# A two-block model step on one core: how the head normalises its inputs, how keys, values and gates are projected, and where three small steps of the feed-forward tail stand

## The reference, cut to what matters

```python
ada_x = split(silu(c) @ w_ada + b_ada, 6);  ada_c = split(silu(c_ctx) @ w_ada + b_ada, 6)
hc = rmsnorm(ctx, g) * (1 + ada_c[1]) + ada_c[0]       # modulated inputs
hx = rmsnorm(x, g)   * (1 + ada_x[1]) + ada_x[0]
pc = hc @ w_in[:, q|k|v|gates] + b_in                  # keys, values, gates of both streams
px = hx @ w_in + b_in
h = sin(z @ w1 + b1); h = sin(h @ w2 + b2); h = h @ w3 # filter chain, 256 x 2048
k = concat(h_forward * decay, h_backward * decay)      # its spectrum multiplies that of the input
...
x = x + g_f * ((silu(gt) * up) @ w_ffn_out)            # twice; the last result is the output
```

## Time and profile before

| | |
|---|---|
| median of three runs (lowest, highest) | 2293.68 us (2292.12, 2294.32) |
| the profiled execution: its own time, its span | 2291.01 us, 2289.2 us |
| busy: TensorE, its weight loads, DVE, ACT | 1917.2 (84%), 1260.9 (55%), 694.3 (30%), 337.6 (15%) us |
| chain that ended last: TensorE, DMA, DVE, ACT | 59%, 33%, 5%, 1% |
| HBM read | 646.10 MB, 283 GB/s over the span |
| 600 to 900 us (experts): DMA share, rate | 1.01, 429 GB/s |

### The profile page before, as it was taken

The page is one execution under the profiler, slowest core; times in us unless marked ns, Lnnn a source line. Parts: engine busy times, 40 slices in busy tenths (PEclk is TensorE's granted clock), DMA queues, the critical chain, the costliest instruction groups (busy, mean ns, idle before and its releaser), DMA issues.

```text
span 2289.2 us, 29892 instructions
## 1 busy us (share of the span) xinstructions
PE 1917.2 (84%) x12646; PEld 1260.9 (55%) x12646; DVE 694.3 (30%) x1643; ACT 337.6 (15%) x776; POOL 0.2 (0%) x4
## 2 busy tenths in 40 slices
PE   7999998966666666666666679999999999999998
PEld 4468687621111111111111137868889978688888
DVE  4113234300000000000000025562656545625554
ACT  3231021200000000000000010260210102602100
POOL 0000000000000000000000000000000000000000
PEclk9999999987878878787878789999999999999999
DMA  9245568999999999999999995524644555246441
GB/s 351 78 146 208 207 246 296 403 429 427 429 428 428 429 428 427 430 427 430 427 430 427 429 405 180 173 75 166 239 165 163 183 189 183 76 166 239 155 158 56
DMA packets 147883, 648.60 MB, mean 283 GB/s; under 512 B 10645, under 2 KB 17410, under 8 KB 123016
## 3 DMA queue, kind: packets, MB, share of 16 engines
q1 hardware_dynamic: 143956, 643.74, 71.1%
q10 hardware_dynamic: 3828, 3.43, 0.5%
HBM read 646.10 MB, written 1.05 MB: 283 GB/s over the span
## 4 chain that ended last, share of the span: by engine, by line
PE 59%; DMA 33%; DVE 5%; ACT 1%; issue 1%; SPq 0%; ACTq 0%; DVEq 0%
DMA ring<-in_w_exp 33%; PE bank L1842 15%; PE bank L825 14%; PE bank L2525 5%; PE bank L1625 4%; PE bank L1377 4%; PE bank L2440 2%; PE bank L1640 2%; PE bank L839 1%; PE bank L858 1%; PE bank L703 1%; DVE scr L2351 1%; PE bank L595 1%; PE bank L1302 1%; PE bank L1311 1%
## 5 line engine op out<-in xcount | busy, mean ns | idle before, releaser
L1625 PE MATMUL bank<-ring,arena 128*32 128x512 f32 x1968 | 309.3, 763 | 205.1 <-DMA ring<-in_w_exp 194.8
L825 PE MATMUL bank<-hx,ring 128*128 128x256 f32 (+1 forms) x1408 | 322.3, 390 | 0.7 <-ACT hx L721 0.7
L1625 PEld LDWEIGHTS bank<-ring,arena 128*32 128x32 f32 x1968 | 61.1, 124 | 436.0 <-DMA ring<-in_w_exp 315.6
L825 PEld LDWEIGHTS bank<-hx,ring 128*128 128x128 f32 x1408 | 267.8, 191 | 53.3 <-issue 18.8
L1640 PE MATMUL bank<-ring,arena 128*32 128x512 f32 x1008 | 157.9, 765 | 81.8 <-DMA ring<-in_w_exp 71.0
L1683 DVE COPY arena<-bank 128x256 f32<-128x256 f32 x16 | 6.8, 425 | 523.8 <-PE bank L1630 523.8
L1842 PE MATMUL bank<-arena 128*128 128x256 f32 x672 | 151.0, 379 | 0.3 <-DVE arena L1891 0.3
L1640 PEld LDWEIGHTS bank<-ring,arena 128*32 128x32 f32 x1008 | 32.1, 129 | 191.6 <-DMA ring<-in_w_exp 113.7
L1842 PEld LDWEIGHTS bank<-arena 128*128 128x128 f32 x672 | 127.0, 190 | 17.5 <-DVE arena L1891 0.6
L1690 DVE COPY arena<-bank 128x256 f32<-128x256 f32 x16 | 6.8, 425 | 343.5 <-PE bank L1514 343.5
L1842 PE MATMUL bank<-ring,hx 128*128 128x256 f32 x448 | 105.8, 379 | 0.0
(11 more groups left out here) (446 smaller groups left out, 2224.7 us busy)
## 6 DMA issues: line engine op xcount, KB each, us to landing
ring<-in_w_exp SPq DMA_DIRECT2D x186, 2048.0 KB, 16.2
ring<-in_w_ada SPq DMA_DIRECT2D x36, 2048.0 KB, 12.1
ring<-in_w_in SPq DMA_DIRECT2D x29, 2048.0 KB, 8.9
ring<-in_w_ffn_in SPq DMA_DIRECT2D x20, 2048.0 KB, 8.0
ring<-in_w_ffn_out SPq DMA_DIRECT2D x10, 2048.0 KB, 7.7
ring<-in_w_out SPq DMA_DIRECT2D x6, 2048.0 KB, 10.9
arena<-in_w_exp SPq DMA_DIRECT2D x4, 2048.0 KB, 19.3
ring<-in_w_up_nsa SPq DMA_DIRECT2D x2, 2048.0 KB, 7.8
```

The costliest lines, as they stand in the source:

```text
L825: ins = pe.matmul(b[:, o:o + n], w[:, k, j * P:(j + 1) * P], h[:, k, :], start=k == 0, stop=k == KD - 1)
L1625: ins = pe.matmul(banks[s][32 * j:32 * j + 32, :], e_xe[:, 2 * t + kk, :], w[:, kk, 512 * j:512 * j + 512], start=t + kk == 0, stop=t + kk ...
```

## The change

Seven edits in one. (1) The head's squares are summed by ACT on the token rows as they arrive (`act_stats`), the rows are scaled there (`act_normed`), and only then turned (`turnxn`, `turncn`); `x` is also turned raw, since it is needed later. The sums over ones on TensorE are gone. ACT modulates `x` and DVE `ctx` in one operation a block. (2) The identity matrix is loaded first, and the filter's tables are issued at the start by ACT. (3) The filter chain is ahead of the tables and the modulation; the taps come in an order that completes the first filter early; five spectra stand ahead of the modulation, two within it, three behind it. (4) Keys and values are made by seven half-size products each (`pe_seven_wide`), with DVE making T and S and combining the results. (5) The gate products go to four column groups of TensorE, and the picks of the gates' rows do too, behind the queries. (6) `dve_late` stands ahead of the second tile's sums. (7) In the last tile of `pe_down` m5 stands ahead of m7, and only one quarter of the result is turned ahead of the last products. The core of the diff:

```diff
+        load("load_ident", ident[:, :], A["k_ident"])
...
-    def act_dft_loads(act):
         act_load(act, "load_decay", decay, A["k_decay"])
         act_load(act, "load_dft", skips, A["hy_skip"].rearrange("a o n -> a (o n)"))
...
+    def dve_gate_pad(v):
+        DV.stage("project")
+        v.wait_ge(*K.loaded("load_ident"))
+        v.memset(wgate, 0.0).then_inc(*DV.step())
+        v.memset(bgate, 0.0).then_inc(*DV.step())
+        v.tensor_tensor(fold0, ident[:, 0:32], ident[:, 32:64], ALU.add).then_inc(*DV.step())
+        for i in (64, 96):
+            v.wait_ge(*DV.last())
+            v.tensor_tensor(fold0, fold0, ident[:, i:i + 32], ALU.add).then_inc(*DV.step("gate pad"))
...
+        for c, a in TAPS:
+            key = f"filter h{c}{a}"
+            v.wait_ge(*at("full " + key))
+            b = bank_of(key)
+            v.tensor_tensor(hfil[:, c, a, :], b[:, :], decay[:, c, a % 2, :], ALU.mult).then_inc(*DV.step("free " + key))
+            if a % 2:
+                o = a // 2
+                v.wait_ge(*DV.last())
+                v.tensor_tensor(hsd[c][o][:, 0, :], hfil[:, c, a - 1, :], hfil[:, c, a, :], ALU.add).then_inc(*DV.step())
...
+            if t == 2:
+                pe_spectra(pe, 1, (0, 1))
+                PE.stage("ada")
...
+    def act_stats(act, src, load, i):
+        AC.stage("stats")
+        act.wait_ge(*K.loaded(load))
+        for c in range(NC):
+            junk = (mg[:, 1024:2048], mg[:, 2048:3072], mg[:, 3072:4096], scr[:, 0:1024])[i + c]
+            act.activation(junk, src[:, c, :], ACT.Square, accum_out=st[:, i + c:i + c + 1]).then_inc(*AC.step("stats"))
...
+    def act_normed(act, key, src, i, read):
+        AC.stage("stats")
+        act.wait_ge(*at("stats scale"))
+        act.wait_ge(*at(read))
+        for c in range(NC):
+            act.activation(src[:, c, :], src[:, c, :], ACT.Identity, scale=st[:, 4 + i + c:5 + i + c]).then_inc(
+                *AC.step(f"{key} normed"))
...
+    def act_modulate_x(act):
+        AC.stage("norm")
+        act.wait_ge(*at("gain mix0"))
+        for k in range(KD):
+            act.activation(hcx[:, k, N:2 * N], scrx[:, k, :], ACT.Identity, bias=adaX[0][:, k:k + 1],
+                           scale=gs[:, k:k + 1]).then_inc(*AC.step("hx done"))
+    def dve_modulate_c(v):
+        DV.stage("norm")
+        v.wait_ge(*at("turncn in3"))
+        for k in range(KD):
+            v.tensor_scalar(hcx[:, k, 0:N], scrc[:, k, :], gsC[:, k:k + 1], adaC[:, k:k + 1], ALU.mult, ALU.add).then_inc(
+                *DV.step("hc done"))
...
+    def pe_seven_wide(pe, key):
+        w = tile(pe, key + "0")
+        T1, T2, T3, T4 = wide_t[key]
+        S1, S2, S3, S4 = wide_s
+        def product(name, b, h, x, first=False, bias=None):
+            for j in range(2):
+                o = b[:, j * 256:(j + 1) * 256]
+                for k in range(4):
+                    start = first and j == 0 and k == 0
+                    if key == "k":
+                        ins = pe.matmul(o, x[:, k, j * P:(j + 1) * P], h[:, k, :], start=start, stop=True, skip_group_check=True)
+                    else:
+                        ins = pe.matmul(o, h[:, k, j * P:(j + 1) * P], x[:, k, :], start=start, stop=True, skip_group_check=True)
+                if key == "v" and bias is not None:
+                    ins = pe.matmul(o, ones[0:1, 0:P], bvrow[:, 256 * bias:256 * bias + 256], start=False, stop=True,
+                                    skip_group_check=True)
+            ins.then_inc(*PE.step(f"m{name} {key}"))
+        r1 = bank(pe, f"{key}r1")
+        product(1, r1, wide_part(0, 0), quarter(w, 0, 0), True)
+        pe.wait_ge(*at("S project"))
+        pe.wait_ge(*at(f"T4 {key}"))
+        r2 = bank(pe, f"{key}r2")
+        product(6, r2, S2, T2, True)
+        r3 = bank(pe, f"{key}r3")
+        product(5, r3, S1, T1, True, 1)
+        pe.wait_ge(*at(f"u2 {key}"))
+        product(7, r2, S3, T3)
+        pe.wait_ge(*at(f"m1 copied {key}"))
+        product(2, r1, wide_part(0, 1), quarter(w, 1, 0), False, 0)
+        pe.wait_ge(*at(f"u3 {key}"))
+        product(4, r2, wide_part(1, 1), T4, False, 0)
+        pe.wait_ge(*at(f"c22 {key}"))
+        product(3, r3, S4, quarter(w, 1, 1))
+        mark_used(pe, key + "0")
...
+    def dve_wide_s(v):
+        S1, S2, S3, S4 = wide_s
+        v.wait_ge(*at("hc done"))
+        v.wait_ge(*at("hx done"))
+        v.tensor_tensor(S1, wide_part(1, 0), wide_part(1, 1), ALU.add).then_inc(*DV.step())
+        s1 = DV.last()
+        v.tensor_tensor(S3, wide_part(0, 0), wide_part(1, 0), ALU.subtract).then_inc(*DV.step())
+        v.wait_ge(*s1)
+        v.tensor_tensor(S2, S1, wide_part(0, 0), ALU.subtract).then_inc(*DV.step())
+        v.wait_ge(*DV.last())
+        v.tensor_tensor(S4, wide_part(0, 1), S2, ALU.subtract).then_inc(*DV.step("S project"))
...
+        v.wait_ge(*at(f"m1 copied {key}"))
+        v.wait_ge(*at(f"m6 {key}"))
+        v.tensor_tensor(wu2, b2, wm1, ALU.add).then_inc(*DV.step(f"u2 {key}"))
+        after(0)
+        after(1)
+        v.wait_ge(*at(f"m7 {key}"))
+        v.tensor_tensor(wu3, b2, wm1, ALU.add).then_inc(*DV.step(f"u3 {key}"))
+        v.wait_ge(*at(f"m5 {key}"))
+        v.wait_ge(*at(f"u3 {key}"))
+        put(1, 1, b3, wu3, f"c22 {key}")
+        after(2)
+        after(3)
+        v.wait_ge(*at(f"m4 {key}"))
+        put(1, 0, b2, wm1, f"free {key}r2", f"c21 {key}")
+        v.wait_ge(*at(f"m3 {key}"))
+        put(0, 1, b3, wu2, f"free {key}r3", f"{key} sums")
...
         pe.wait_ge(*at("hx done"))
-        pe_linear_T(pe, "k", "k0", hcx, 512)
-        w = tile(pe, "v0")
-        for s in range(2):
-            for c in range(NC):
-                b = bank(pe, f"v{s}{c}")
-                for k in range(KD):
-                    pe.matmul(b[:, :], hcx[:, k, s * N + c * P:s * N + (c + 1) * P], w[:, k, :], start=k == 0,
-                                  stop=False)
-                pe.matmul(b[:, :], ones[0:1, 0:P], bvrow, start=False, stop=True).then_inc(*PE.step(f"full v{s}{c}"))
-        mark_used(pe, "v0")
+        pe_seven_wide(pe, "k")
+        pe_seven_wide(pe, "v")
+        pe.wait_ge(*K.loaded("load_gate"))
         b = bank(pe, "gates")
         for k in range(KD):
-            ins = pe.matmul(b[0:16, :], wgate[:, k, :], hcx[:, k, :], start=k == 0, stop=k == KD - 1)
+            q = 32 * (k % 4)
+            ins = pe.matmul(b[q:q + 32, :], wgate[:, k, :], hcx[:, k, :], start=k < 4, stop=k >= 4)
         ins.then_inc(*PE.step("full gates"))
-        pe.wait_ge(*at("gates16"))
-        for g in range(4):
-            b = bank(pe, f"gate{g}")
-            pe.matmul(b[0:4, :], ident[0:16, 4 * g:4 * g + 4], gate16, start=True, stop=True).then_inc(*PE.step(f"full gate{g}"))
         x = hcx[:, :, N:2 * N]
         pe_linear_T(pe, "q", "q0", x, N)
+        pe.wait_ge(*at("gates summed"))
+        b = bank(pe, "gate rows")
+        for g in range(4):
+            ins = pe.matmul(b[32 * g:32 * g + 4, :], fold0[:, 4 * g:4 * g + 4], gate4, start=True, stop=True)
+        ins.then_inc(*PE.step("full gate rows"))
...
+        for i in range(4):
+            dve_wide_t(v, "k", i)
+        dve_wide_s(v)
         v.wait_ge(*at("full spec14"))
         v.memset(vx[:, :, :, P:P + 1], 1.0).then_inc(*DV.step())
         v.memset(vc[:, :, :, P:P + 1], 1.0).then_inc(*DV.step())
         v.memset(r_s[:, 7, :], 0.0).then_inc(*DV.step("v ones"))
+        dve_seven_wide(v, "k", lambda i: dve_wide_t(v, "v", i))
         dve_conv(v, 0)
+        dve_seven_wide(v, "v", lambda i: None)
         dve_conv(v, 1)
         dve_rows(v)
         dve_conv(v, 2)
...
                 product("m6", m, T2, S2)
+                product("m5", m, T1, S1)
                 product("m7", m, T3, S3)
-                product("m5", m, T1, S1)
-                product("m4", m, T4, down_part(m, 1, 1))
                 if l == LAYERS - 1:
                     pe_result(pe, 0, 0)
-                    pe_result(pe, 1, 1)
                     PE.stage("ffn")
+                product("m4", m, T4, down_part(m, 1, 1))
                 product("m3", m, q[1, 1], S4)
...
+        v.wait_ge(*at(f"dn{l}m5 5"))
+        v.tensor_tensor(dv2, b["m5"][:, :], du2, ALU.add).then_inc(*DV.step())
+        v.wait_ge(*DV.last())
+        to_x(dv2, 0, 1, False)
         v.wait_ge(*at(f"dn{l}m7 5"))
         v.tensor_tensor(du3, b["m7"][:, :], du2, ALU.add).then_inc(*DV.step(f"free dn{l}m7"))
         v.wait_ge(*DV.last())
-        v.wait_ge(*at(f"dn{l}m5 5"))
-        v.tensor_tensor(dc22, b["m5"][:, :], du3, ALU.add).then_inc(*DV.step())
+        v.tensor_tensor(dc22, b["m5"][:, :], du3, ALU.add).then_inc(*DV.step(f"free dn{l}m5"))
         v.wait_ge(*DV.last())
         to_x(dc22, 1, 1, True)
...
+        dve_late(v, 3 * l + 2)
+        DV.stage("ffn")
         for m in range(1, 6):
             dve_down_s(v, l, m)
             for i in range(4):
                 dve_down_t(v, l, m, i)
-            if m == 1:
```

(45 more changed lines are left out.)

205 lines of the change are left out of this document (123 added, 82 removed).

## The result

The changed kernel takes 2277.03 us (median of four runs, 2274.85 to 2279.31), 0.9932 of the kernel before, with a 95% interval of 0.9919 to 0.9944: 0.7% faster, which is 15.6 us of 2293.68 (the plain medians differ by 16.65). The forecast was 2270 with a gain of 23.8, and a range of 2262 to 2285. So the time lies in the range, but outside the likeliest case's own 2265 to 2275. The profiled execution took 2277.35, its span is 2275.5 us, 13.7 less than before.

What follows compares the result with a forecast made beforehand. TensorE was taken to bound nearly everything, leading the experts' weight stream. 16.5 us before the experts plus 7.3 in the tail, 23.8 off 2291.0, gave 2267.2; the runs' median stands 2.7 higher, so 2270, range 2262 to 2285.

Steps and rivals of the forecast that it cites:

- the likeliest case: Whole kernel: 23.8 us gained, giving 2270, with 2265 to 2275 of its own; chance 0.55.
- the clock's term: Keys: one stretch of low granted clock at the 4.8 us wait for S, 1.7 us; bounds none or three.
- The wait for silu: Head: silu of the condition stands behind the first five spectra's evictions, ends at 42.5, turned and copied at 43.3.
- short bias row: Values: a bias row of 256 columns takes 0.7 us, six take 4.2; bounds 2.6 and 6.7.
- the rival of the later head: Head: taps on VectorE wait for filter tables landing at 26, shifting everything up to S by 7 us; 2275 to 2285, chance 0.24.
- a second stretch: Within the later-head rival: one more stretch of low clock, adding 2 us.
- what matters is one moment: Head: the second key product's start, which waits for VectorE's last sum S, done at 68.9 us after a 4.8 us wait.
- the gates: Between values and queries: gate products in four column groups take 2.0 us, where gates and their rows took 11.4.
- the tail: Expert down-projection's end in both layers: earlier late step 3.6, m5 ahead of m7 2.6 and 1.1; 7.3 us together.
- the queries and picks: Before the next modulation: queries 14.0 us and picks in four groups 1.3, the picks behind the queries.
- the hidden combinations: Keys and values: VectorE's combinations hide beside TensorE's products; bare they would cost some 2 us a tile.
- the stream follows: Experts: the weight stream is led by TensorE, so the stretch shifts as a whole; rival, early gain lost, 2286, chance 0.05.

Runs made afterwards that it cites:

- experiment 4: Kernel after plus eleven extra unread products filling TensorE's 4.93 us wait for VectorE's last sum S in the keys; 2274.15 us, ratio 0.9913.
- experiment 1: Kernel after plus eight extra unread products in TensorE's idle stretch between the second filter product and the taps; 2270.89 us, ratio 0.9900.
- experiment 3: Kernel after with silu of the condition and the tables' turn moved ahead of the first five spectra; 2271.64 us, ratio 0.9901.
- experiment 9: Kernel after with edits 1 to 3 undone: the old head under the new keys, values, gates and tail; 2266.64 us, ratio 0.9885.
- experiment 11: Kernel after with early silu, and tables and modulation ahead of all ten spectra; 2262.93 us, ratio 0.9868.
- experiment 5: Kernel after with the old tail: late step behind the second tile's sums, m7 ahead of m5, two quarters turned early; 2285.66 us, ratio 0.9965.
- experiment 6: Kernel after with the old gates: 16 columns of weights in one column group, picks ahead of the queries; 2288.31 us, ratio 0.9977.

## Why the prediction came out as it did

The head's terms, as put and as measured in the kernel after (the forecast added its 1.7 us of low clock only at the last row; it isn't in those of the keys and values):

| step | forecast | measured |
|---|---|---|
| VectorE can start the taps | 19.3 | 20.13 |
| its taps and sums end | 30.9 | 33.5 |
| turns of ctx end | 31.7 | 37.4 |
| five spectra end | 40.3 | 46.0 |
| modulation starts | 43.3 | 49.3 |
| modulation's last tile ends | 54.6 | 62.4 |
| gains | 56.1 | 64.8 |
| S done | 68.9 | 77.7 |
| keys end | 89.6 | 100.1 |
| values end | 118.0 | 129.2 |
| next modulation | 137.0 | 146.1 |

The step of the sum that failed is the clock's term: "I take one such stretch there, 1.7 us", in the keys alone. That stretch was there and cost 1.4 in the kernel after (experiment 4). What I left out is the idle time ahead of the taps. The forecast knew from its own times that TensorE would have nothing to do between the second filter product and 17.7 us, and asked about the clock only in the keys. By the end of the turns 5.7 us were missing, and experiment 1, which fills that idle time, gives 5.3 of them back. The wait for silu (forecast inside 43.3) brought another stretch, 1.7 in the modulation, shown by experiment 3, which loses the wait and the stretch together. Two spectra's evictions ahead of the last row's copy on ScalarE (62.41 [chain above]) added 0.9. Of the 9.1 us missing at the next modulation these are 8.3; the values' 29.1 against 28.4 is most of the rest. The 0.7 that a short bias row was to take by the earlier trace rows was 0.62 in the chain.

The time fell where the rival of the later head had it, 2275 to 2285, but by another way. Its tables did hold VectorE up, by 1.06 us (20.13 is when the last landed, not 26). What decided is the low clock, which the rival had only as "a second stretch" at 2 us; the one in the taps and turns cost more than twice that. So the range held by the width of this rival, and the likeliest sum missed the gain before the experts by more than half (7.5 for 16.5). That is luck as much as judgement.

A deeper fault does not show in the sum. The forecast said that "what matters is one moment", the last S, and compared its 68.9 with nothing. The head of before, with the new keys under it, reaches that moment at 69.5 and starts the keys' combinations with no wait at all (experiment 9), since its modulation stands ahead of the spectra and VectorE works beside them. I credited the whole difference between 153.56 and 137.0 to the change, where the early head took 10.8 us away. Putting T and S behind the spectra was the loss; the same row squares and normalised turns with the modulation first gave 14.7 (experiment 11), 3.9 more than the old head.

What held: the gates (10.3 measured, 9.7 by the terms), the tail (7.6 by the ratio, 8.0 by the two traces, 7.3 forecast; its three terms of 3.6, 2.6 and 1.1 each show in the traces of experiment 5), the queries and picks (14.01 and 0.97, forecast 14.0 and 1.3), VectorE's 12.8 us from the gains to S (12.9), the hidden combinations (from 77.78 to 129.24 the chain is TensorE's without a gap), and that the stream follows: a gain of 7.5 at the next modulation was 5.8 at the first expert transfer, the other 1.7 lost in a stretch of low clock ahead of it (27.86 for a step that took 29.55 in this execution). The table load of 1.28 had its silu 0.02 behind it again (46.65 and 47.95); the further drain that the Trainium skill gives ("ScalarE: Activation LUTs", What ACT_TABLE_LOAD costs) does not show here either.

Experiments 1, 3 and 4 gain 2 to 4 us more over the whole than their traces show up to 146 us. By the end of the expert stretch the traces have 6.2, 5.7 and 3.7 us, against 7.3, 7.1 and 4.4 by the ratios. In each, 1.7 is the stretch of low clock at 353 us, which the profiled execution of the kernel after has and theirs have not (29.55 against 27.86; six of the fourteen profiled executions have it, and no run shows why). The remainder is within the intervals.

Left open: why the same wait for S costs 1.4 us of low clock in some executions and 3.0 in others, and why the taps stay at the low level for 14 us.

## What to carry to other kernels

Before an edit that starts work earlier, list the idle stretches that it leaves on TensorE, and price each with the slow work behind it: 3.65 idle us cost 6.9 in the taps here, 5.3 of them at the next step. A scheme that moves work to VectorE paid here only where TensorE had other work to do in that time, so place it beside such work first and count saved products second. And compare a new order with the old order under the same other edits, not with the old kernel: here three edits lost 10.8 us inside a change that won 15.6.

## What the runs showed of the hardware that was not expected

- In all eight kernels whose stretch ahead of the taps was idle (3.4 to 3.65 us), the sixteen records of the taps took 13.95 to 14.0 us, 1054 to 1057 ns each at the median; with it filled, three had 589 or 590 ns, and the fourth, with fillers between the taps, 641. The low level lasted 14 us of busy TensorE through the taps and came back up in the turns behind them. Behind other waits, where products with 128 rows of weights followed, it cost less: 1.4 to 1.7 us behind 2.34, 1.6 behind 3.32 (3.47 against 1.88), 1.4 to 3.0 behind 4.93 to 5.03. The kernel before had such a wait too, ahead of its sums over ones:

```profile
21.24 8.83 PE L703 MATMUL bank<-scr,ones 128*128 128x256 f32 x32 [3.80 <-ACT scr L710]
```

  At experiment 4's pace (20.98 for 96 such records) 32 take 7.0, so 3.80 idle us cost 1.8 there, where 3.65 ahead of the taps cost 6.9. No run tells whether it is the 64 rows of the taps' weights that makes the difference.
- The column of the granted clock can be wrong. The windows of experiment 11 from 20 to 28 us, and the same line's view:

```profile
20.00:24.00 4.00, 4.00 (x6) 1.58 (x5) 3.25 (x6) 3.98 (x5) 0.00 (x0) 1.00 1.05 387
24.00:28.00 4.00, 4.00 (x5) 1.38 (x5) 3.21 (x6) 1.17 (x2) 0.00 (x0) 1.00 1.05 388
```

```profile
L451 PE MATMUL bank<-hx,arena x16: 1053/1055/1187, 17.6 to 30.6; 64*128 64x512 f32 x16
```

  The column says full clock, the records take what they take at 0.50. The profile of experiment 6 has the same (1.00 from 16 to 36 us, and 13.99 us for the taps). The duration of a known product is the safer witness.
- An activation with an accumulated sum has a second record of 0.19 to 0.20 us behind it (ScalarE, 128x1024 squares at 1.04 to 1.07).
